# Value products of attention grouped by four steps, the first transfers halved over two queues, and a last unit of 256 columns

## What is computed

```
h = x @ w_in + b_in                       # 1024 -> q k v z_a u_g v_g z_g g_a g_g
y_a = sliding_window_attention(q, k, v, sinks) * silu(z_a)   # 8 query heads, 2 key heads, 64 wide
y_g = chunked_spatial_gating(gelu(u_g), gelu(v_g), ...) * silu(z_g)
merged = sigmoid(g_a) * (y_a @ w_branch_attn) + sigmoid(g_g) * (y_g @ w_branch_gmlp)
x = layer_norm(ALPHA * x + merged @ w_out + b_out)
```

## Time and profile before

| | |
|---|---|
| median of three runs | 1581.36 us |
| the profiled execution | 1581.76 us |
| its span | 1580.0 us |
| TensorE busy | 1567.5 us (99%), 12961 matmuls |
| VectorE, ScalarE, GpSimd busy | 989.1, 603.4, 379.7 us |
| wide products, lines 396 to 398 of x alone | 619.5 + 608.8 + 609.0 us |
| DMA | 141.12 MB, mean 89 GB/s |

### The profile page before, as it was taken

How to read it: one execution, slowest core, us unless ns; L and a number is a source line. 1 busy time by engine, 2 the same in 40 slices (tenths; PEclk the granted TensorE clock), 3 DMA queues, 4 the chain that set the end, 5 groups by cost and what they waited for, 6 DMA issues and landing times.

```text
span 1580.0 us, 31192 instructions
## 1 busy us (share of the span) xinstructions
PE 1567.5 (99%) x12961; PEld 1401.6 (89%) x12961; DVE 989.1 (63%) x1534; ACT 603.4 (38%) x1102; POOL 379.7 (24%) x349
## 2 busy tenths in 40 slices
PE   9999999999999999999999999999999999999998
PEld 8999999999989898899998898888888988888887
DVE  6665565765866668576685577566616775665346
ACT  5323222353354344335445455473112256541121
POOL 0000000020421224041241124337430043363510
PEclk9999999999999999999999999999999999999999
DMA  5323223223212312222222142222223322222331
GB/s 167 108 80 107 81 85 103 81 81 113 82 55 68 96 55 82 85 77 60 76 82 95 55 132 81 80 81 81 85 102 134 117 90 80 81 80 80 108 132 54
DMA packets 113675, 141.12 MB, mean 89 GB/s; under 512 B 2972, under 2 KB 90432, under 8 KB 113536
## 3 DMA queue, kind: packets, MB, share of 16 engines
q1 hardware_dynamic: 109056, 133.60, 26.1%
q10 hardware_dynamic: 4400, 5.32, 1.1%
q0 software_dynamic: 80, 0.20, 0.0%
HBM read 137.01 MB, written 2.10 MB: 88 GB/s over the span
## 4 chain that ended last, share of the span: by engine, by line
PE 98%; DVE 1%; DMA 0%; issue 0%; ACT 0%; ACTq 0%
PE acc L396 28%; PE acc L398 28%; PE acc L397 28%; PE aux L537 2%; PE aux L396 1%; PE aux L398 1%; PE aux L397 1%; PE aux L1332 1%; PE aux L602 1%; PE aux L604 1%; PE aux L524 1%; PE aux L1319 1%; PE aux L594 1%; DMA xt<-in_x 0%; PE aux L1358 0%; PE aux L614 0%
## 5 line engine op out<-in xcount | busy, mean ns | idle before, releaser
L396 PE MATMUL acc<-xhis,whi 128*128 128x264 f32 (+2 forms) x1872 | 619.5, 331 | 0.4 <-DVE xlos L2177 0.2
L398 PE MATMUL acc<-xhis,wlo 128*128 128x264 f32 (+2 forms) x1872 | 609.0, 325 | 0.0
L397 PE MATMUL acc<-xlos,whi 128*128 128x264 f32 (+2 forms) x1872 | 608.8, 325 | 0.0
L396 PEld LDWEIGHTS acc<-xhis,whi 128*128 128x128 f32 x1872 | 352.5, 188 | 33.8 <-issue 4.8
L398 PEld LDWEIGHTS acc<-xhis,wlo 128*128 128x128 f32 x1872 | 352.4, 188 | 29.4
L397 PEld LDWEIGHTS acc<-xlos,whi 128*128 128x128 f32 x1872 | 352.8, 188 | 26.7
L391 POOL TENSOR_TENSOR wlo<-raw,whi 128x1024 fp32r<-128x1024 f32 x84 | 207.5, 2471 | 363.7 <-DVE whi L2414 363.7
L387 ACT ACTIVATE whi<-raw 128x1024 fp32r<-128x1024 f32 x158 | 164.1, 1048 | 131.7 <-PE acc L398 119.6
L391 DVE TENSOR_TENSOR wlo<-raw,whi 128x1024 fp32r<-128x1024 f32 x81 | 99.8, 1235 | 37.7 <-ACT whi L387 37.5
L2118 DVE TENSOR_TENSOR wlo<-raw,whi 128x1024 fp32r<-128x1024 f32 x77 | 93.8, 1220 | 22.4 <-ACT whi L387 22.2
L2414 DVE CAST whi<-raw 128x1024 fp32r<-128x1024 f32 x84 | 70.1, 838 | 54.0 <-PE acc L398 53.9
(11 more groups left out here) (371 smaller groups left out, 2803.3 us busy)
## 6 DMA issues: line engine op xcount, KB each, us to landing
raw<-in_w_in SPq DMA_DIRECT2D x38, 1024.0 KB, 5.1
raw<-in_hgrn_w_in SPq DMA_DIRECT2D x32, 1024.0 KB, 5.6
raw<-in_pool_w_in SPq DMA_DIRECT2D x15, 1024.0 KB, 5.5
raw<-in_pool_w_out SPq DMA_DIRECT2D x8, 1024.0 KB, 5.0
raw<-in_hgrn_w_out SPq DMA_DIRECT2D x8, 1024.0 KB, 5.0
raw<-in_w_out SPq DMA_DIRECT2D x8, 1024.0 KB, 5.0
raw<-in_pool_w_grp SPq DMA_DIRECT2D x4, 1024.0 KB, 5.2
raw<-in_w_branch_attn SPq DMA_DIRECT2D x4, 1024.0 KB, 4.9
```

Source lines behind the costliest of these rows:

```text
L396: pe.matmul(dst, stat[0], mov[0], start=first, stop=False)
L397: pe.matmul(dst, stat[0], mov[1], start=False, stop=False)
L398: return pe.matmul(dst, stat[1], mov[0], start=False, stop=last)
```

## The change

Three things. The opening's transfers: the first two quarters of x and the first weight piece are halved and asked for by both queues; high and low parts read the turned tile itself in PSUM, the copies to `h` come later, and the turns of feature tiles 2 and 3 stand between the first products of unit 0 and of unit 1. `WARM` is 8 instead of 6, and the idle products are 5 instead of 13. `LAST` is 256 instead of 384. In attention, the value products of four steps stand together at the front of visits 6, 10, 14 and 18; `pt` has four buffers, of which the two new ones lie where `brow` was, and ScalarE waits for what it would overwrite.

```
-WARM = 6
+WARM = 8
-LAST = 384
+LAST = 256
...
-            brow = sb("brow", [P, D], where=before_g)
+            with ExitStack() as in_rows:
+                brow = sb("brow", [P, D], where=in_rows)
+            pt_more = [sb(f"pt{s}", [P, 4, P], where=before_g) for s in (2, 3)]
...
+            x_part(slice(2 * P, SEQ), slice(0, 2 * P), x_landed[0])
             sp.dma_start(ident[:, :], a["c_ident"]).then_inc(first_landed, 16)
             sp.dma_start(rows1[NW0:FNW, :], a["norm_w"].rearrange("l (k p) -> (l k) p", p=P))\
...
+            first_chunk(2, 4, first_half)
+            x_part(slice(2 * P, SEQ), slice(2 * P, 4 * P), x_landed[1])
+            first_chunk(4, KT, raw_landed[0])
+            for n in (2, 3):
+                x_part(slice(0, SEQ), slice(2 * P * n, 2 * P * n + 2 * P), x_landed[n])
...
-                idle(3)
+                pe.wait_ge(first_landed, 32)
                 turn(0)
+                first_rows()
                 turn(1)
-                idle(4)
+                idle(5)
+                pe.wait_ge(meta_high, 2)
+                pe.wait_ge(half_low, 1)
+                v_products(0, (0, 1))
                 turn(2)
                 turn(3)
-                idle(6)
-                pe.wait_ge(meta_high, 2)
-                for n in range(2):
-                    pe.wait_ge(half_low, n + 1)
-                    v_products(n, (0, 1))
+                pe.wait_ge(half_low, 2)
+                pe.wait_ge(meta_ready, 2)
+                v_products(1, (0, 1))
...
+                for t in range(s - 6, s - 2) if s >= 6 and s % 4 == 2 else ():
+
+                    p, b = ATT[t]
+                    pe.wait_ge(apt_ready, 1 + base + t + 1)
+                    if b == 0:
+                        pe.wait_ge(ya_ready, 1 + 4 * i + p)
+                    for kb_ in range(0 if b else 1, 2):
+                        for x in range(2):
+                            kv = (2 * p + x) // 4
+                            mm = pe.matmul(aux2[HD * x:HD * x + HD, 1, P * b:P * b + P],
+                                           vtc[:, b - 1 + kb_, HD * kv:HD * kv + HD],
+                                           pt[t % 4][:, 2 * x + kb_, :],
+                                           start=(kb_ == (0 if b else 1)), stop=(kb_ == 1))
+                    mm.then_inc(ao_full, 1)
...
-                if 3 <= s:
-
-                    t = s - 3
...
+            act.dma_start(xt[:, 0:2, 0:2 * P], a["x"][0][0:2 * P, 0:2 * P].rearrange("(c p) n -> p c n", p=P))\
+               .then_inc(x_landed[0], 16)
             act.dma_start(mt[:, :], a["meta_tokens"]).then_inc(meta_landed, 16)
...
-                    act.activation(pt[z][:, :, :].rearrange("p (x k) q -> p x k q", x=2)[:, :, first:, :],
+                    if t >= 4:
+                        act.wait_ge(ao_full, base + t - 3)
+                    if t == 2:
+                        act.wait_ge(res_ready, 4 * i + 4)
+                    act.activation(pt[t % 4][:, :, :].rearrange("p (x k) q -> p x k q", x=2)[:, :, first:, :],
```

More of the change, by code:

```diff
@@ L277, in program @@
             pr = [sb(f"pr{s}", [P, 2, 2 * P + 1], where=before_m) for s in range(2)]
-            pt = [sb(f"pt{s}", [P, 4, P], where=before_m) for s in range(2)]
+            pt = [sb(f"pt{s}", [P, 4, P], where=before_m) for s in range(2)] + pt_more
             sgc = [xn[0][:, 0:SEQ], rstd[:, 0:SEQ]]
@@ L856, in const, with x_part, first_chunk @@
                 sp.dma_start(dst, src).then_inc(const_landed, 16)
+            def x_part(rows, cols, landed):
+                sp.dma_start(xt[:, rows.start // P:rows.stop // P, cols],
+                             a["x"][0][rows, cols].rearrange("(c p) n -> p c n", p=P)).then_inc(landed, 16)
+            def first_chunk(k0, k1, landed):
+                sp.dma_start(raw[0][:, 256 * k0:256 * k1].rearrange("p (k n) -> p k n", n=256),
+                             w_in_a[:, k0:k1, 0:256]).then_inc(landed, 16)
+            x_part(slice(2 * P, SEQ), slice(0, 2 * P), x_landed[0])
             sp.dma_start(ident[:, :], a["c_ident"]).then_inc(first_landed, 16)
@@ L1040, in _ @@
                 pe.matmul(aux[:, n % 2, 0:P], ones_d[:, :], ones_d[:, :], start=True, stop=True)
[L1041 to L1047, removed]
             def idle(n):
@@ L1054, in turn @@
                 if k % 2 == 0:
-                    pe.wait_ge(x_landed[k // 2], 16)
+                    pe.wait_ge(x_landed[k // 2], 16 if k >= 4 else 32)
                 if k >= 4:
@@ L1060, in turn, with first_rows @@
                 mm.then_inc(xt_turned, 1)
+            def first_rows():
+                pe.wait_ge(first_landed, 32)
+                pe.transpose(acc[0][:, 0, NW0:FNW], rows1[NW0:FNW, :], ident[NW0:FNW, NW0:FNW]).then_inc(vec_full, 1)
+                pe.wait_ge(meta_landed, 16)
+                for k in range(KT):
+                    mm = pe.transpose(acc[1][:, 0, META * k:META * k + META], mt[:, P * k:P * k + P],
+                                      ident[0:META, 0:META])
+                mm.then_inc(meta_turned, 1)
             def vectors():
@@ L1474, in _ @@
             act.sem_inc(on_ready, 1)
+            act.dma_start(xt[:, 0:2, 0:2 * P], a["x"][0][0:2 * P, 0:2 * P].rearrange("(c p) n -> p c n", p=P))\
+               .then_inc(x_landed[0], 16)
             act.dma_start(mt[:, :], a["meta_tokens"]).then_inc(meta_landed, 16)
-            for n in range(3):
-                cols = slice(2 * P * n, 2 * P * n + 2 * P)
-                act.dma_start(xt[:, :, cols], a["x"][0][:, cols].rearrange("(c p) n -> p c n", p=P))\
-                   .then_inc(x_landed[n], 16)
+            act.dma_start(raw[0][:, 0:512].rearrange("p (k n) -> p k n", n=256), w_in_a[:, 0:2, 0:256])\
+               .then_inc(first_half, 16)
+            act.dma_start(xt[:, 0:2, 2 * P:4 * P], a["x"][0][0:2 * P, 2 * P:4 * P].rearrange("(c p) n -> p c n", p=P))\
+               .then_inc(x_landed[1], 16)
             def row_squares(half, tiles):
                 cols = slice(4 * P * half, 4 * P * half + 4 * P)
-                act.wait_ge(x_landed[2 * half + 1], 16)
+                act.wait_ge(x_landed[2 * half + 1], 16 if half else 32)
                 for c in tiles:
@@ L1873, in x_low @@
                 dve.wait_ge(xhi_ready, k + 1)
-                dve.scalar_tensor_tensor(out=xlo[:, k, META:T], in0=h[:, k, META:T] if k < 4 else x_turned(k),
+                dve.scalar_tensor_tensor(out=xlo[:, k, META:T], in0=x_turned(k),
                                          scalar=vec1[:, NW0 + k:NW0 + k + 1], in1=xhi[:, k, META:T],
@@ L1895, in _ @@
             half_lo(1)
[L1896 to L1897 removed]
+            dve.tensor_copy(h[:, :, 0:META], meta_psum).then_inc(meta_ready, 1)
+            x_copied(0)
+            x_copied(1)
             x_low(2)
@@ L1901, in _ @@
             rest_lo(1)
+            x_copied(2)
+            x_copied(3)
             x_low(4)
```

35 lines of the change are left out of this document (11 added, 24 removed).

## The result

The changed kernel took 1570.49 us, the median of four runs from 1569.45 to 1572.97, against 1581.78 for the kernel before in the same session: ratio 0.9932, 95% interval 0.992 to 0.9944. That is 11.3 us faster. The forecast was 1566.7 with its own range 1565.0 to 1568.5, and 1564.5 to 1571.0 for eight in ten: the sign and most of the size are right, the single value is 3.8 us too low, and the result lies above the narrower range and near the upper end of the wider one. The profiled execution is the fastest of the four, 1569.45 us with a span of 1567.6, so in the two traces 12.4 us lie between the spans where 14.7 were forecast.

The account below looks back on a forecast made before the run. TensorE, holding 98% of the chain of work, was taken as the bound. The terms 8.7 + 2.9 + 2.3 + 0.8 = 14.7 us came off 1581.36, giving 1566.7, range 1565.0 to 1568.5 (eight in ten: 1564.5 to 1571.0).

Parts of the forecast that it names:

- Grouped value products: Attention: merging four steps' value products into one group saves entering and leaving; 8.7 us, bounds 7.5 to 9.3.
- small term for "zg": Attention: in two places a longer visit covers the first "zg" unit's wait for VectorE; 0.35 us.
- no wait would be named before scores: Attention, expected new profile: 8 groups of 28 records, about 1.9 us each, no wait named before scores or transposes.
- the 6.5 that I had named as a sign of being wrong: Attention: the prediction is wrong if visits without products are over 6.5 us apart.
- the softmax chain's cover at step 4: Attention: step 4's probabilities are scaled at 992.49, TensorE wants them two visits on, 12 us; priced at nothing.
- The edge of an instruction packet: Hgrn stage: shifting instructions by 23 removes a burst's stop of 1.49 us, twice; 2.9 us, bounds -3.0 to 3.0.
- the count of the new places: Hgrn stage: after the shift, the nearest bursts begin 27, 38 and 42 instructions past a packet's edge.
- one stop all the same: Rival, hgrn stage: the packet's edge still stops a burst; 1569.6, or 1572.5 with one more stop pair; chance 0.22.
- The opening: Start of kernel: halved, earlier transfers bring the first product to 8.2 us; gain 2.3 us, bounds 0.8 to 2.8.
- My own sign of being wrong: Opening: the prediction is wrong if the first product stands after 9.5 us; it was expected near 8.3.
- The last unit: End of kernel: two times 256 columns win 1.1 us, VectorE's tail loses 0.26; net 0.8, bounds 0.5 to 1.0.
- The rival on borders: Attention: borders between steps inside a group cost as much as leaving it; 8.3 us come back, 1575.0; chance 0.06.

Follow-up runs that it names:

- v_two: a_vec with value products in groups of two steps in every second visit instead of four in every fourth, 16 groups instead of 8; 1571.90 us, ratio 0.9937.
- v_vg: a_vec with VectorE's aggregation of the norm of v_g behind the attention work of unit zg 1, not ahead of that unit's read-out; 1569.06 us, ratio 0.9919.
- e_shift: The kernel before without 6 warming products and with one more waiting instruction, so later TensorE instructions move by 23; 1581.02 us, ratio 0.9992.
- a_back: The changed kernel with 23 more waiting TensorE instructions in the opening's pause, putting later instructions back where they stood before; ratio 0.9949, runs 1572.96 to 1574.24 us.
- e_open: The kernel before with the new opening alone, and with it the shift of later TensorE instructions by 23; 1580.02 us, ratio 0.9987.
- a_again: The changed kernel unaltered, run and traced once more; ratio 0.9934 to the kernel before, runs 1569.91 to 1572.51 us.
- a_warm: The changed kernel with 10 warming products instead of 8 and 3 idle ones instead of 5; ratio 0.9927, runs 1570.05 to 1570.89 us.
- a_vec: The changed kernel with small vectors and their transposes ahead of x again, 6 warming and 7 idle products; ratio 0.9925, runs 1569.10 to 1570.47 us.
- e_group: The kernel before with the grouped value products alone; 1573.74 us, ratio 0.9953.
- e_last: The kernel before with a last unit of 256 and 256 columns alone; 1580.97 us, ratio 0.9989.

## Why the prediction was right or wrong

**What bounds the kernel** was right: TensorE's stream alone, as all parts add up and no edit to another engine counted unless TensorE waited for it.

**Grouped value products** (8.7 forecast, 7.9 measured, within the bounds of 7.5 to 9.3). The mechanism and the price of a group hold: 0.34 from rows, 0.33 from v_two. So does the small term for "zg". The longer visit 10 covers the unit's wait for VectorE's read-out and gives 0.18 us in each layer, 0.35 as forecast: from the last product before the visit to the next unit it is 1.77 us before, where visits 6 and 14 have 1.60, and 2.71 in all three with the change. One step failed. I said that no wait would be named before scores. In visit 12 VectorE is late, because 1.6 us of the norm's aggregation stand ahead of its attention work and the visits are shorter now; that costs 0.47 us a layer, 0.93 in all, which is the whole miss of this term. It also makes this visit 6.88 us long, over the 6.5 that I had named as a sign of being wrong. I had measured the softmax chain's cover at step 4, in a visit without the norm, and took it for all. v_vg shows both the cause and the remedy. The Trainium skill ("TensorEngine Tiling (Array Packing)", "Key Properties") says that a change of tiling mode drains the engine; v_two agrees in kind, with 0.33 us a group.

**The edge of an instruction packet** (2.9 forecast, 2.6 in the trace, 1.2 to 2.4 in seven other traces with the new places). The inference held: two kernels that change the places and not the transfers (e_shift, a_back) take the loop's stops away and bring them back, and the packets' own times fit. What failed is the count of the new places. I took the nearest to be 27, 38 and 42 past an edge. The one that stops is another, the first burst behind the loop, 36 ahead of an edge in my count, and its stop sits 107 of 128 records into it: my count is off once the loop is left, and I had no row from which to see that. Why it is off isn't shown. The stop came in seven of the eight traces with these places, at 0.9 to 1.2 us of named wait, and in the profiled execution of the changed kernel as a smaller one at 758.72 instead. That the trace comes within 0.3 us of this term is therefore partly luck. The rival "one stop all the same" had 0.22 and was nearer to the truth. The Trainium skill ("Runtime: NRT & Kernel Launch", "Instruction fetch mechanics") calls such crossings "mostly hidden": mostly is right for the other bursts, but these, of 256 instructions in 1.2 us, stop for 0.9 to 1.6 us of named wait.

**The opening** (2.3 forecast, 1.0 in the trace, a loss of 1.1 to 1.5 in the three other traces of this opening: e_open, a_again, a_back). This is the step that failed. I put the landing of the small vectors at 4.6 us, "behind 320 KB of their queue instead of 64", with a bound of 5.4; it was 5.6 to 5.9 in these four traces and in a_warm, beyond the bound. The chain behind it was near, 9.6 - 5.76 = 3.8 us where I had 3.6. But it held a second gap: I gave the landing of the first weight piece no place in the sum, and it landed at 8.1 and ended the wait for the first product, 1.45 us later. Had the vectors come at 4.6 and the weights still at 8.1, the first product would have stood at 9.6 all the same and not at 8.2. My own sign of being wrong, a first product after 9.5, came true. a_vec gives back what was lost: vectors at 3.7, weights at 6.85, first product at 8.67, and 1.95 us gained at the 25th. And I did not see that TensorE's clock was part of the opening: the kernel before has it up by 4.7 us in three of three traces, the changed one in one of four.

**The last unit** (0.8 forecast, 0.85 in the trace): 5.7 us long as said.

**The sum.** Of the 3.8 us by which the median missed, 1.3 are the opening in its good state, 0.8 the attention and 0.3 the packets' edges, all in the trace; 1.0 is what the median run is longer than the profiled one, which had the early clock and the smaller stop behind the loop (that the median run lacked one of them is likely and not shown, since it has no trace); 0.4 is what I had taken off for the median before. The rival on borders has a slip that changes nothing: 24 x 0.35 is 8.4, not 8.3.

## What to carry to other kernels

When a transfer is moved ahead of a small one, price the small one's landing from rows with the new bytes ahead of it on both queues, and ask which chain starts there: 72 KB behind 256 KB landed 1.6 us later, and with the old order of the small ones the halved pieces gave twice as much (1.95 us against 1.04). Ask the same of every other piece that the chain needs, here the weights. When visits get shorter, look for the visit with the most other work on each helper engine, not for a typical one. Where a program has bursts of a packet's length, a change of a few instructions far ahead moves the time by 1 to 3 us, and a comparison of two kernels has to be cleared of it, and of the moment when TensorE's clock comes up.

## What the runs showed of the hardware

- A burst of 128 tiny matmuls stops for 1.2 to 1.8 us between two records when the program ahead of it has one length, in every trace with that length (before, e_group, e_last, a_back), and not with 23 instructions fewer, in any of the others. Behind the loop it is the other way round, in seven traces of eight. A stopped burst goes on 1.2 to 1.5 us after the landing of an instruction packet that started just ahead of it, in fifteen stops of fifteen.
- The granted clock is 1.00 in the profile in stretches where like products stand 0.22 us apart and in others where they stand 0.12 apart. Only the distances show that TensorE starts at 1.2 GHz; the step came between 3.9 and 13.8 us.
- 23 instructions that wait for a semaphore long raised cost 0.44 us in the middle of a stream of wide products.
- A group of half-width products costs 0.33 to 0.34 us to enter and leave, and steps inside it nothing that can be seen.
